# Attention units in another order, and VectorE empties the transposes of the short ones

## What is computed

```
# latent attention, prompt: blocks of 128 queries, each reads all frames of its chunk and earlier ones
s = where(mask, (q_nope . k_nope + q_rope . kpe) * MLA_SCALE, -1e30)
p = softmax(s);  out = p @ v                  # 8 heads, 4 blocks of queries
# latent attention, sample: 8 streams, 128 cached frames + 16 new ones, 8 heads
p = softmax(logits(q, concat(cache, new)));  out = p @ v
# window attention, sample: the same 144 keys and a learned sink per head
```

## Time and profile before

| | |
|---|---|
| median of 3 timed runs | 919.78 us (918.79 to 921.39) |
| the profiled execution | 920.1 us, span 918.3 us |
| TensorE busy | 880.5 us, 96% of the span |
| VectorE, ScalarE busy | 485.5 us (53%), 390.5 us (43%) |
| granted TensorE clock | 0.997 of full speed on average |
| attention stage | 292.40 to 369.62 us |

### The profile page before, as it was taken

One profiled execution on the slowest core, in us unless ns is written; L12 is line 12 of the kernel. 1 busy time (PEld: TensorE's weight loads), 2 busy tenths in 40 slices (PEclk: granted clock), 3 DMA queues, 4 the chain that ended last, 5 costly groups with the idle time before them and its releaser, 6 DMA issues.

```text
span 918.3 us, 13750 instructions
## 1 busy us (share of the span) xinstructions
PE 880.5 (96%) x5457; PEld 799.9 (87%) x5457; DVE 485.5 (53%) x745; ACT 390.5 (43%) x771; POOL 75.8 (8%) x73
## 2 busy tenths in 40 slices
PE   4999999999999988999999899999999999999997
PEld 3888899989977776998878899999999998888885
DVE  5523522433344555564668877777777774343124
ACT  5311422244454556452565544445545443332112
POOL 0300198050030000000000000000000000000000
PEclk9999999999999999999999999999999999999999
DMA  6523246062240000654623232223333226322202
GB/s 266 162 87 79 73 112 202 8 188 83 76 106 1 1 1 2 184 176 180 217 92 92 69 90 74 78 82 92 93 92 92 76 86 223 98 69 92 70 24 115
DMA packets 101452, 91.92 MB, mean 100 GB/s; under 512 B 8480, under 2 KB 85296, under 8 KB 101248
## 3 DMA queue, kind: packets, MB, share of 16 engines
q1 hardware_dynamic: 95072, 85.93, 30.3%
q10 hardware_dynamic: 5424, 3.25, 1.2%
q0 software_dynamic: 896, 1.92, 0.6%
HBM read 79.60 MB, written 12.40 MB: 100 GB/s over the span
## 4 chain that ended last, share of the span: by engine, by line
PE 91%; ACT 3%; DVE 3%; DMA 1%; issue 1%; DVEq 0%; ACTq 0%
PE ps L1142 27%; PE ps L1144 26%; PE ps L1143 26%; PE ps L1316 2%; PE ps L1365 1%; PE ps L1327 1%; PE ps L1412 1%; PE ps L1286 1%; PE ps L1359 1%; PE ps L1290 1%; DVE nm_c L1687 1%; ACT probs L871 1%; PE ps L1389 1%; PE ps L1399 1%; DMA x_t<-in_x_prompt 1%
## 5 line engine op out<-in xcount | busy, mean ns | idle before, releaser
L1624 DVE TENSOR_TENSOR wlo<-raw,whi 128x1024 fp32r<-128x1024 f32 x59 | 77.4, 1315 | 212.1 <-ACT whi L800 204.6
L800 ACT ACTIVATE whi<-raw 128x1024 fp32r<-128x1024 f32 x59 | 62.0, 1056 | 178.6 <-PE ps L1144 169.6
L1142 PE MATMUL ps<-h_hi,wlo 128*128 128x320 f32 x288 | 90.9, 316 | 1.9 <-DVE z L1664 1.0
L1144 PE MATMUL ps<-h_hi,whi 128*128 128x320 f32 x288 | 89.0, 309 | 0.0
L1143 PE MATMUL ps<-h_lo,whi 128*128 128x320 f32 x288 | 88.9, 309 | 0.0
L1142 PE MATMUL ps<-sc_hi,t_lo 128*128 128x320 f32 x252 | 78.0, 309 | 3.9 <-ACT u L1057 2.9
L1144 PE MATMUL ps<-sc_hi,t_hi 128*128 128x320 f32 x252 | 77.8, 309 | 0.0
L1143 PE MATMUL ps<-sc_lo,t_hi 128*128 128x320 f32 x252 | 77.8, 309 | 0.0
L1047 ACT ACTIVATE t_hi<-wd 128x512 fp32r<-128x512 f32 x84 | 52.8, 629 | 58.6 <-DVE wd L1883 52.8
L1142 PE MATMUL ps<-whi,gu_lo 128*128 128x512 f32 x190 | 74.0, 390 | 0.3 <-DVE gu_lo L1955 0.3
L1143 PE MATMUL ps<-wlo,gu_hi 128*128 128x512 f32 x190 | 73.9, 389 | 0.0
(11 more groups left out here) (302 smaller groups left out, 2135.4 us busy)
## 6 DMA issues: line engine op xcount, KB each, us to landing
raw<-in_w_gate_up SPq DMA_DIRECT2D x44, 512.0 KB, 3.8
raw<-in_w_down SPq DMA_DIRECT2D x22, 512.0 KB, 3.7
raw<-in_w_in SPq DMA_DIRECT2D x16, 512.0 KB, 4.0
raw<-in_w_in SPq DMA_DIRECT2D x12, 480.0 KB, 4.3
gates_scratch<-gate_s SPq DMA_DIRECT2D x16, 320.0 KB, 2.4
gate_r<-gates_scratch SPq DMA_DIRECT2D x8, 640.0 KB, 4.0
raw<-in_w_branch SPq DMA_DIRECT2D x8, 512.0 KB, 4.7
raw<-in_w_out SPq DMA_DIRECT2D x8, 512.0 KB, 5.6
```

The lines of the kernel that those rows point to most:

```text
L800: act.activation(whi[:, r % 2, :] if to is None else to, raw[:, r, :], ACT.Copy).then_inc(w_hi, 1)
L1142: pe.matmul(out, left[1], right[0], start=first, stop=False, skip_group_check=not own_group)
L1144: return pe.matmul(out, left[0], right[0], start=False, stop=last, skip_group_check=not own_group)
L1624: dve.tensor_tensor(lo[:, place, :], raw[:, r, :], hi[:, place, :].bitcast(F32), ALU.subtract).then_inc(w_lo, 1)
```

## The change

The order of units is another. Before: four pairs (mla_s, p3), four pairs (p2, swa_s), four pairs (p1, p0). Now: four pairs (mla_s, p0), four pairs (p2, swa_s), four pairs (p3, p1). The turned probabilities of window units and of p0 and p1 are copied out of PSUM by VectorE; mla_s, p2 and p3 stay with ScalarE. One semaphore becomes two, `pt_act` and `pt_dve`, with counts by engine.

```diff
 for n in range(4):
-    UNITS += [("mla_s", n, 0), ("mla_p", 3, n)]
+    UNITS += [("mla_s", n, 0), ("mla_p", 0, n)]
...
 for n in range(4):
-    UNITS += [("mla_p", 1, n), ("mla_p", 0, n)]
+    UNITS += [("mla_p", 3, n), ("mla_p", 1, n)]
...
+def turned_by_dve(u):
+    kind, a, _ = UNITS[u]
+    return kind == "swa_s" or (kind == "mla_p" and a < 2)
+def turned_count(u):
+    return sum(turned_by_dve(v) == turned_by_dve(u) for v in range(u + 1))
...
+        def pt_copied(eng, u):
+            eng.wait_ge(pt_dve if turned_by_dve(u) else pt_act, turned_count(u))
...
             def pt_copy(u):
                 w = unit_width(u)
+                if turned_by_dve(u):
+                    return
...
                 if turned_before(u) is not None:
-                    pe.wait_ge(pt_rdy, turned_before(u) + 1)
+                    pt_copied(pe, turned_before(u))
...
-                pe.wait_ge(pt_rdy, u + 1)
+                pt_copied(pe, u)
...
-                pe.wait_ge(o_hi, 4)
+                pe.wait_ge(o_hi, ENDED.index(("mla_s", 3)) + 1)
...
+            def pt_copy(u):
+                w = unit_width(u)
+                if not turned_by_dve(u):
+                    return
+                dve.wait_ge(pt_full, u + 1)
+                if u >= 2:
+                    dve.wait_ge(pv_done, u - 1)
+                dve.tensor_copy(probs_T[:, u % 2, 0:2 * w], ps[:, turn_banks(u)[0], 0:2 * w]).then_inc(pt_dve, 1)
...
                 if 1 <= i < NU + 1:
                     normalise(i - 1)
+                if 2 <= i < NU + 2:
+                    pt_copy(i - 2)
```

More of the change, by code:

```diff
@@ L457, in build_layer @@
             sem(n) for n in ("probs_rdy", "s_full", "s_nm", "s_exp", "s_inv", "s_norm"))
-        pt_full, pt_rdy, pv_done, o_hi, o_lo = (
-            sem(n) for n in ("pt_full", "pt_rdy", "pv_done", "o_hi", "o_lo"))
+        pt_full, pt_act, pt_dve, pv_done, o_hi, o_lo = (
+            sem(n) for n in ("pt_full", "pt_act", "pt_dve", "pv_done", "o_hi", "o_lo"))
         c_full, c_nm, c_exp, c_inv, c_norm = (sem(n) for n in ("c_full", "c_nm", "c_exp", "c_inv", "c_norm"))
@@ L880, in pt_copy @@
                     act.activation(probs_T[:, u % 2, 0:2 * w].rearrange("p (c n) -> p c n", c=2), ps[:, 4:6, 0:w],
-                                   ACT.Copy).then_inc(pt_rdy, 1)
+                                   ACT.Copy).then_inc(pt_act, 1)
                 else:
-                    act.activation(probs_T[:, u % 2, 0:2 * w], ps[:, turn_banks(u)[0], 0:2 * w], ACT.Copy).then_inc(pt_rdy, 1)
+                    act.activation(probs_T[:, u % 2, 0:2 * w], ps[:, turn_banks(u)[0], 0:2 * w], ACT.Copy).then_inc(pt_act, 1)
             def o_evac(u):
```

## The result

The changed kernel takes 929.49 us (median of 4 executions, 928.46 to 931.6) against 920.5 for the kernel before (the three executions of the prediction and one more): ratio 1.0107, 95% interval 1.0082 to 1.0132. It is slower. The forecast was 927.6 and a ratio of 1.0085. The profiled execution took 928.62 us with a span of 926.8, 8.5 more than before.

The account below looks back on a forecast made before the run. TensorE, busy for 96% of the span, was taken as the bound. Waits of 14.67 less 8.36 before gave +6.3 us, the clock's fall 1.5, so +7.8: span 926.1, median 927.6, range 924.8 to 929.9.

Parts of the forecast that it names:

- only waits change: Attention stage: same 24 units, so TensorE's work stays the same; only waits go from 8.36 to 14.67 us.
- the clock's fall: Behind the bank 6 wait, TensorE drops once to 1.2 GHz after idling, costing 1.5 us of a possible 1.7.
- stall = need - cover: TensorE's wait is scores' end to next turn's start (need) minus TensorE's work in between (cover).
- The three p3 turns: p3 with p1 pairs: turns wait for p3's copy, need 3.96, cover 2.43; stalls 1.53 twice and 1.51 once.
- The window pairs: p2 with swa_s: four turns wait for wide copies, 1.21, 0.96, 0.97 and 1.42, together 4.56 us.
- Bank 6: First p3 outputs must wait until the window group leaves this PSUM bank: 2.66 us.
- Start and first units: Start and mla_s with p0 pairs: waits for exps and ScalarE's copies, 1.63 at the start, 1.25 after.
- The copies on VectorE: Twelve copies moved from ScalarE: taken as 0 on TensorE's path, at worst +8.3 us.
- (a): Rival: the same stalls in the attention stage but no fall of the clock, 926.1 us; chance 0.36 together with (d).
- (b): Rival: not slower; ScalarE, rid of twelve copies, cuts p3's need from 3.96 to 2.43; 920.1 or 918.7 us; chance 0.05.
- (c): Rival: VectorE's copies come late behind the next unit's normalising, p1's outputs wait; 3.6 us more, 931; chance 0.06.
- (d): Rival: bank 6 is emptied in time for half its price, 926 us; chance 0.36 together with (a).

Follow-up runs that it names:

- experiment 5: Changed kernel with ScalarE's copies of three- and four-tile units moved ahead of the exps of the unit two steps later: 922.11 us, ratio 1.0027.
- experiment 6: Kernel before, order and copy engines kept, with only the wide copies moved ahead of the exps on ScalarE: 915.18 us, ratio 0.9954.
- experiment 7: Kernel before with a third order of units (equal units often adjacent) and no other edit, copies still on ScalarE: 913.52 us, ratio 0.9943.
- experiment 3: Changed kernel with output banks of four-tile and two-tile prompt units exchanged, so p3 follows p2 in bank 7: 925.41 us, ratio 1.0074.
- experiment 1: Changed kernel's order of units, with all copies of turned probabilities on ScalarE as before: 927.98 us, ratio 1.0094.
- experiment 2: Old order of units, with the short units' copies on VectorE: 918.35 us against 918.69 for the kernel before, ratio 0.9991.
- experiment 4: Changed kernel with 20 useless identity transposes into idle bank 7 where TensorE waits for os_lo: 926.69 us, ratio 1.0082.
- experiment 9: Changed kernel again, unedited, with a second profile: 928.57 us, ratio 1.0118 to the kernel before.
- experiment 8: Kernel before with the third order of units and wide copies ahead of the exps, all copies on ScalarE: 911.89 us, ratio 0.9915.
- experiment 10: Changed kernel with exchanged output banks and wide copies ahead of the exps: 916.83 us, ratio 0.9979 to the kernel before.

## Where the prediction was right, and which of its steps failed

The direction, the places and the mechanism were right. What failed are sizes in the sum: the change of the stage was forecast at +7.8 and measured at +9.15. The waits of the start and the first eight units were too small (2.88 forecast, 3.63 measured), "only waits change" put the change of TensorE's other work at nothing (+0.63 measured), and the clock's fall was taken at 1.5 (1.7 measured).

*The rule "stall = need - cover".* It stood. The three p3 turns were to wait 1.51, 1.53, 1.53, and waited 1.25, 1.28, 1.28 by the profile, 1.40 to 1.43 in the prediction's way of counting. Their need was 3.97 (p3's scores end at 342.93, the turn starts at 346.90), forecast 3.96; what was 0.1 too small is p3's own turn in the cover (0.97 for 0.87), so the pair took as long as forecast. The window pairs: 1.21, 0.96, 0.97, 1.42 forecast; 1.21, 0.96, 0.96, 1.41 measured. Experiments 5 and 6 shortened the need and the waits went; experiment 7 lengthened the cover and they went too.

*Bank 6.* 2.66 forecast, 2.71 measured; experiment 3 removed it alone.

*Start and first units.* This term failed: 1.63 and 1.25 forecast. Measured 0.97, 0.20, 0.39 and 0.24, 0.24, 0.69, with 0.15 on each 2.01 and 1.62: 0.75 more. The needs were right; the covers were too long, for the most part by p0's turn. TensorE's timeline of the changed kernel, from a sample unit's turn to its outputs:

```profile
300.64 0.60 PE L1344 MATMUL ps<-ident,probs_m 128*128 128x128 f32 x4
...
301.54 0.71 PE L1333 MATMUL ps<-k_T,q_T 128*128 128x128 f32 x4
302.09 0.38 PE L1344 MATMUL ps<-ident,probs 128*128 128x128 f32 x2
```

The outputs follow at 302.71, so the need is 2.07, just as forecast. But the turn of p0 that was put at "about 0.37, half of the four transposes' row with its tail, rounded up", ends at 302.71 - 0.24 = 302.47, 0.38 after its start; with the 0.15 of tail taken off it is 0.23 us. That makes each of these two waits 0.39 in place of 0.25. The third was to have a cover of 2.24 and had 2.13 (0.84 in place of 0.75). At the start the first wait was 1.12 in place of 1.02, and the cover of the first outputs 1.19 in place of 1.46, since the turns of the sample unit and of p0 and p0's scores were each 0.08 to 0.10 shorter. The 0.89 that it lacked, in place of 0.61, are two waits: 0.20 for VectorE's normalising, which the prediction didn't list, and 0.39. The price of p0's turn stood in the trace of before too (TensorE's timeline, ahead of an idle 0.41 that ends at 351.66, so 0.24 by the same working):

```profile
350.86 0.38 PE L1327 MATMUL ps<-ident,probs 128*128 128x128 f32 x2
```

*"The units are the same, so TensorE's work is the same. Only waits change."* This step failed. By the prediction's counting the fourteen waits are 13.06 + 14 x 0.15 = 15.16 us, and the fall took 1.72; that leaves 69.49 of the stage where before had 77.22 - 8.36 = 68.86: 0.63 more. Experiment 3, which has no fall, gives 0.75 in the same way. Start-to-start, a sample unit's outputs take 1.89 instead of 1.79, now that each follows a wait, and the first scores behind one take 0.1 longer (row of 0.76 instead of 0.65); p3's turns take 0.97 instead of 0.87, ahead of other blocks than before. Why a block takes longer there is not shown. The group of half of these outputs by line and form, with the mean ns of one, in the kernel before:

```profile
L1359 PE MATMUL ps<-probs_T,c_ckv 128*128 128x128 f32 x32 | 6.2, 275 | 0.0
```

And in the changed kernel, where the idle time before it has appeared as well:

```profile
L1376 PE MATMUL ps<-probs_T,c_ckv 128*128 128x128 f32 x32 | 6.6, 288 | 1.6 <-ACT probs_T L900 1.6
```

*The copies on VectorE.* Taken as 0 on the path. Experiment 1 confirms it for this order; in the old order the move gave 0.6 us (experiment 2). Their own time was that of the nearest rows (groups by line and form; 0.692 was to be expected from the earlier trace rows):

```profile
L1723 DVE COPY probs_T<-ps 128x512 f32<-128x512 f32 x8 | 5.5, 688 | 4.5 <-PE ps L1344 4.5
...
L1723 DVE COPY probs_T<-ps 128x256 f32<-128x256 f32 x4 | 1.7, 418 | 0.0
```

ScalarE's copies of 128x512 took 0.600. This agrees with the Trainium skill, "VectorE: DVE Perf Modes", section "Specifications", which has ScalarE closer to PSUM. The difference costs nothing where nobody waits for the copy.

*The clock.* The fall came where it was forecast and cost 1.7 (1.72 in experiment 4), where 1.5 was taken: nearly all of it landed on the p3 scores (3.68 instead of 1.98), which nothing covers.

*The sum.* Stage: 6.3 forecast without the clock, 7.4 measured; with it 7.8 and 9.15, a seventh too small. The first stretch adds 0.75, the other work 0.63 and the clock 0.2; the waits of the p3 pairs take 0.26 back. In the median, 927.6 forecast and 929.49 measured, the 1.9 us are made up so: +1.35 from the stage, -0.65 from the rest of the program, and +1.2 because the forecast took over from before that the median lies 0.3 below the profiled execution, where it lay 0.9 above. The last two go with the clock's falls elsewhere, of which the forecast took no account: in experiment 9 the median of four was 928.57. The base was uncertain by as much: a first median of before of 919.78, and 918.4 to 918.9 later. The range's upper end doesn't follow from its own words: 927.6 + 14 x 0.15 is 929.7, not 929.9, and the list has 13 waits; the fourteenth is the 0.20.

Of the rivals, (a), no fall, is excluded by the granted clock of 0.57 and experiment 4, and its reason, that a fall needs more than the 1.64 us of idling that passed, by experiment 6, where no single idle stretch was longer than 1.13; (b), a shrinking need, by the waits of 1.25 and more; (c), late copies on VectorE, by experiment 1 and the absence of any such wait; (d), bank 6 at half price, by the 2.56. What wasn't tried: a way to give p3's group its bank earlier than experiment 3 does, and copies of wide units shared between both engines.

## What to carry to other kernels

Where engines walk one list in lockstep, price an order by two distances at each block: how long the next one's input takes from the last thing that starts it (need), and how much work its engine has in between (cover). Which unit is long on which engine says little; the sum of the waits says nearly all: with the clock's falls taken out, it forecast the stage of experiments 3, 6, 7, 8 and 10 (70 to 82 us) to within half a microsecond, in 7 and 8 with errors of a half to one that cancelled; in the first forecast it was 1.1 short. So price the short blocks from their own rows too, and not by halving a longer one: in a cover, a tenth of a microsecond is a tenth of wait.

Before moving work to another engine, look at what stands ahead of it in its own queue: moving the eight wide copies ahead of the exps gave 3.8 us in the kernel before, moving twelve copies to VectorE at most 0.6.

And a wait of a few microseconds on TensorE costs more than its length when the lower clock follows it.

## What the runs showed of the clock that was not expected

How long TensorE idled didn't alone decide whether the clock fell. In the profile of before it fell after 2.00 us of idling at 159 to 161 us, and it stayed at 1.00 after 2.92 us at 505 to 508. TensorE's timeline of before there:

```profile
507.98 0.38 PE L1142 MATMUL ps<-sc_hi,t_lo 128*128 128x320 f32 x1 [2.92 <-ACT u L1057]
```

And the window behind it:

```profile
506.00:513.00 7.00, 5.02 (x34) 5.05 (x35) 6.54 (x10) 5.20 (x10) 0.00 (x0) 1.00 0.00 0
```

In the changed kernel it was the other way round: its idle 2.00 near 160 us was followed by a clock of 1.00 and its 2.93 near 515 by 0.72 on average over six microseconds:

```profile
159.00:165.00 6.00, 4.10 (x30) 3.12 (x31) 5.55 (x15) 2.99 (x7) 0.00 (x0) 1.00 0.18 71
514.00:520.00 6.00, 4.70 (x22) 4.73 (x23) 5.54 (x9) 4.19 (x8) 0.00 (x0) 0.72 0.00 0
```

In experiment 6 idle stretches of 0.41, 1.13 and 0.21 within five microseconds came before a fall, and in the kernel before the same ones did not. In experiment 5, with a wait of 4.12, the clock fell before the wait was over and stayed low about twice as long as the others (0.51 over seven microseconds). What decides between two executions of the same stretch stays open; the same kernel's times spread by 3 us, and the falls go with it.
